# Gated delta rule in one block kernel: sums of squares in two other PSUM banks, the last level's mask ahead of the weights and the convolution

## The reference, cut to what matters

```python
qkv = silu(conv5(proj[..., C_QA:C_ZA]))            # depthwise, 5 taps
qa = _l2norm(q) * 128 ** -0.5 ; ka = _l2norm(k)    # x * rsqrt(sum(x*x) + EPS)
kb = kc * bc
a_kk = strict_lower(kb @ kc.T * gam)
sol = triangular_solve(a_kk + eye, [vc*bc, kb*exp(gc)])    # per chunk
...
o = _rmsnorm(o_forward + o_backward, norm_a) * silu(z)
```

## Time and profile before

| | us |
|---|---|
| median of the runs | 2743.36 |
| profiled execution, its own time | 2740.5 |
| its span | 2738.7 |
| TensorE busy in the span | 2316.0 (85%) |
| VectorE busy | 1069.8 (39%) |
| GpSimd busy | 828.6 (30%) |
| ScalarE busy | 705.8 (26%) |

### The profile page before, as it was taken

One profiled execution on the slowest core, in us unless ns is written; L12 is line 12 of the kernel. 1 busy time (PEld: TensorE's weight loads), 2 busy tenths in 40 slices (PEclk: granted clock), 3 DMA queues, 4 the chain that ended last, 5 costly groups with the idle time before them and its releaser, 6 DMA issues. The chain is left out here.

```text
span 2738.7 us, 30202 instructions
## 1 busy us (share of the span) xinstructions
PE 2316.0 (85%) x11455; PEld 1751.5 (64%) x11455; DVE 1069.8 (39%) x1761; ACT 705.8 (26%) x1088; POOL 828.6 (30%) x757
## 2 busy tenths in 40 slices
PE   4999778898869984999994996889997997479995
PEld 3888666776656663788883664678886666334442
DVE  3121356767730035433336453455664114311112
ACT  3333233334212122222222442422221212011110
POOL 2433045565412230544430111244441323000001
PEclk8999889999879997999997999899998999589998
DMA  4422123222004221323213303111101412759995
GB/s 132 107 77 62 35 76 91 62 56 76 24 14 125 81 92 46 123 92 107 92 46 68 78 16 105 35 31 24 25 7 26 133 47 97 312 201 419 417 418 202
DMA packets 283986, 292.86 MB, mean 107 GB/s; under 512 B 77552, under 2 KB 247664, under 8 KB 274224
## 3 DMA queue, kind: packets, MB, share of 16 engines
q1 hardware_dynamic: 271768, 240.58, 27.8%
q10 hardware_dynamic: 6816, 31.46, 2.8%
q0 software_dynamic: 5280, 19.18, 2.0%
HBM read 318.33 MB, written 23.17 MB: 125 GB/s over the span
## 5 line engine op out<-in xcount | busy, mean ns | idle before, releaser
L1983 PE MATMUL moe_bank<-ex_wgu,Y 128*64 128x512 f32 x768 | 171.4, 598 | 3.0 <-ACT Y L2030 1.6
L1352 POOL TENSOR_TENSOR m_wgs<-m_wg,m_wgs 128x1024 fp32r<-128x1024 f32 x32 | 79.4, 2499 | 251.1 <-ACT m_wgs L1388 251.1
L596 PE MATMUL gdn_bank<-hh,gdn_ws 128*128 128x512 f32 x256 | 119.0, 465 | 31.4 <-ACT gdn_rn L1081 24.4
L1983 PEld LDWEIGHTS moe_bank<-ex_wgu,Y 128*64 128x64 f32 x768 | 66.0, 138 | 103.3 <-issue 103.3
L1548 POOL TENSOR_TENSOR ff_wus<-ff_wu,ff_wus 128x2048 fp32r<-128x2048 f32 x16 | 73.8, 4610 | 185.9 <-ACT ff_wus L1606 185.9
L1433 DVE TENSOR_TENSOR m_sg<-m_sg,m_bank 128x512 f32<-128x512 f32 x32 | 22.0, 688 | 275.7 <-ACT m_sg L1396 275.7
L761 POOL TENSOR_TENSOR gdn_ws<-gdn_wr,gdn_ws 128x1024 fp32r<-128x1024 f32 x32 | 76.0, 2377 | 170.3 <-ACT gdn_ws L1032 170.1
L1955 POOL DMA_INDIRECT hT<-token_rows,rows x24 | 22.8, 951 | 344.9 <-PE moe_bank L1968 232.6
L596 PE MATMUL ff_bank<-ff_hh,ff_wus 128*128 128x512 f32 x256 | 101.0, 394 | 13.9 <-POOL ff_wus L1548 13.9
L596 PE MATMUL m_bank<-hh,m_wgs 128*128 128x512 f32 x256 | 106.1, 414 | 0.0
L597 PE MATMUL gdn_bank<-hl,gdn_ws 128*128 128x512 f32 x256 | 105.8, 413 | 0.0
(11 more groups left out here) (516 smaller groups left out, 5814.1 us busy)
## 6 DMA issues: line engine op xcount, KB each, us to landing
ex_wgu<-in_w_gate_e SPq DMA_DIRECT2D x42, 1024.0 KB, 16.5
ex_wgu<-in_w_up_e SPq DMA_DIRECT2D x42, 1024.0 KB, 19.3
ex_wd<-in_w_down_e SPq DMA_DIRECT2D x42, 1024.0 KB, 21.7
Y<-in_w_in SPq DMA_DIRECT2D x48, 512.0 KB, 3.9
gdn_wr<-in_w_in SPq DMA_DIRECT2D x32, 512.0 KB, 4.1
m_wg<-in_w_in SPq DMA_DIRECT2D x32, 512.0 KB, 5.6
ff_wu<-in_w_ff SPq DMA_DIRECT2D x16, 1024.0 KB
ff_wd<-in_w_ff SPq DMA_DIRECT2D x16, 1024.0 KB
```

The source lines that it names most:

```text
L596: pe.matmul(bank, left(0, l), right(0, r), start=(start and n == 0), stop=False)
L1352: pool.tensor_tensor(wgs[:, j, n, 1], wg[:, n], wgs[:, j, n, 0], ALU.subtract).then_inc(s.low, 1)
L1983: ins = pe.matmul(bank[2 + j][half, :], hgT[:, j, k, half], w[:, e, k], start=(k == 0), stop=(k == KT - 1))
```

## The change

The two sums of squares go to banks 4 and 5, which in a period's first third nobody uses, since the chain of the head before has left them. The output's sum of squares goes to bank 4. TensorE's `fill` for a first step in bank 0 then waits for VectorE's convolution of the head before, and in bank 1 for ScalarE's SiLU of z, both from the end of the period before, in place of ScalarE's Ln. The chain's first multiply in direction 1 waits for the Ln of both sums and of the norm. `gram_kq` moves behind `yz_mm(1)`. On VectorE, `take_yz(1)` and `take_x(2)` stand ahead of `weights` and of the first five taps. ScalarE's, GpSimd's and the DMA queue's orders stay.

```diff
@@ fill
                         if b == 0 and g:
-                            pe.wait_ge(s.rnl, 2 * g - 1)
-                        elif b == 1 and g >= 3:
-                            pe.wait_ge(s.orl, g - 2)
+                            pe.wait_ge(s.conv, 3 * g)
                         elif b == 1 and g:
-                            pe.wait_ge(s.rnl, 2 * g)
+                            pe.wait_ge(s.zs, g)
@@ squares(h)
                 pe.wait_ge(s.sq, 2 * h + 1)
-                pe.wait_ge(s.conv, 3 * h + 3)
-                pe.matmul(bank[0][:, :], G.c("ones"), sq[:, 0, :], start=True, stop=True).then_inc(s.ssq, 1)
+                if h == 0:
+                    pe.wait_ge(s.gts, 1)
+                elif h >= 2:
+                    pe.wait_ge(s.r, 6 * (h - 1))
+                    pe.wait_ge(s.vn, 8 * (h - 1))
+                pe.matmul(bank[4][:, :], G.c("ones"), sq[:, 0, :], start=True, stop=True).then_inc(s.ssq, 1)
                 pe.wait_ge(s.sq, 2 * h + 2)
-                pe.wait_ge(s.zs, h + 1)
-                pe.matmul(bank[1][:, :], G.c("ones"), sq[:, 1, :], start=True, stop=True).then_inc(s.ssq, 1)
+                pe.matmul(bank[5][:, :], G.c("ones"), sq[:, 1, :], start=True, stop=True).then_inc(s.ssq, 1)
@@ norm(j)
-                    pe.wait_ge(s.rnl, 2 * (j + 2) + 2)
-                pe.matmul(bank[1][:, :], G.c("ones"), osqb[:, :], start=True, stop=True).then_inc(s.oss, 1)
+                    pe.wait_ge(s.rnl, 2 * (j + 2) + 1)
+                else:
+                    pe.wait_ge(s.r, 6 * (j + 1))
+                pe.matmul(bank[4][:, :], G.c("ones"), osqb[:, :], start=True, stop=True).then_inc(s.oss, 1)
@@ chain, st = 0
+                            if d and h is not None:
+                                pe.wait_ge(s.rnl, 2 * h + 2)
+                            if d and i:
+                                pe.wait_ge(s.orl, i)
@@ TensorE's period
                     fill(g, 3)
+                if i is not None:
+                    yz_mm(i, 1)
                 if h is not None:
                     gram_kq(h)
-                if i is not None:
-                    yz_mm(i, 1)
                 fill(g, 4)
@@ ScalarE
-                        act.activation(rn[:, j, :], bank[j][:, :], ACT.Ln, bias=G.eps[:, 0:1]).then_inc(s.rnl, 1)
+                        act.activation(rn[:, j, :], bank[4 + j][:, :], ACT.Ln, bias=G.eps[:, 0:1]).then_inc(s.rnl, 1)
@@ VectorE's period
                 if i is not None:
                     take_x(i, 1)
+                if i is not None:
+                    take_yz(i, 1)
+                    take_x(i, 2)
                 if h is not None:
                     weights(h)
-                if i is not None:
-                    take_yz(i, 1)
                 convolve(5)
                 if i is not None:
-                    take_x(i, 2)
                     take_yz(i, 2)
                     chain(i)
```

More of the change, by code:

```diff
@@ L1088, in _ @@
                     act.wait_ge(s.oss, p)
-                    act.activation(ornb[:], bank[1][:, :], ACT.Ln, bias=G.eps[:, 0:1], scale=1.0 / P).then_inc(s.orl, 1)
+                    act.activation(ornb[:], bank[4][:, :], ACT.Ln, bias=G.eps[:, 0:1], scale=1.0 / P).then_inc(s.orl, 1)
                     act.wait_ge(s.orl, p)
```

## The result

The changed kernel takes 2749.55 us (median of 20 runs, 2743.71 to 2759.41) against 2742.84 us of the kernel before in the same comparison (20 runs): a ratio of 1.0023, 95% interval 1.0013 to 1.0032. It is some 6 us slower, 0.2%: less than the 8 us that the prediction took as its bound, and yet clear of no change.

A forecast was written before the change was run, and what follows sets the result against it. TensorE was taken to bound the kernel. Full periods -2.0, period p = -1 -2.2 and the clock +3.6 sum to -0.6 us, carried to the median of 2743.4: 2743 us, range 2731 to 2754.

The forecast's parts named there:

- the 8 us that the prediction took as its bound: Whole kernel's time: about 0.3% is what a measurement here can tell from no change.
- The exchange of waits: TensorE, full periods: three waits of 6.76 us become 0.7 (`gram_kk`), 0.7 (`x_mm(1)`), 2.0 (`yz_mm(1)`), 4.3 (`turn_v`); about 0.2 gained.
- VectorE's collision with GpSimd's split: VectorE's mask behind the taps: 2.77 us beside GpSimd's split, forecast to take the 0.69 it needs alone.
- Period p = -1: Period ahead of the full ones: first step no longer waits for Ln, `solve` starts earlier; -2.2 us, between 1.5 and 3.1.
- the tail: From p = 6 on: no gain, since its last head waits 5.1 us for the inverse by DMA, whose chain starts unchanged.
- +3.6 us for the clock: TensorE behind `turn_v`: clock falls as often as before, 13 us in all, of which 9.4 lay there before.
- the likeliest case: Whole kernel: waits are exchanged, no change, within -8 to +8 us; chance 0.67.
- -2.0: Six full periods without the clock term: -0.6, -0.9 and -0.5 us together; bounds +1.5 and -5.
- the upper bound of +9.3: TensorE's clock behind `turn_v`: the long fall every time, 6 x 3.1 = 18.7 us in place of 9.4.
- the taps that come later still: Rival: slower TensorE ahead of `take_x(2)` delays taps, SiLU, copy, `turn_v`; up to 1.7 us a period, +15 in all; chance 0.12.
- The prediction's row for the clock behind the wait for Ln: TensorE's granted clock behind that wait before the change: 1.00 four times, 0.66 over 5 us twice.

The follow-up runs named there:

- the idle matmuls: Changed kernel plus 7 matmuls nobody reads ahead of `yz_mm(1)` in the six full periods; ratio 1.0007 to the kernel before.
- the copies first: Changed kernel with ScalarE's `ktok` and `vtok` copies ahead of part k's SiLU and Square; ratio 0.9966 to the kernel before.
- the banks and the swap: Kernel before with the new banks and `gram_kq` behind `yz_mm(1)`, VectorE's order as before; ratio 1.0001, 2743.7 us.
- two steps early: Changed kernel with two of the four projection steps behind `gram_kq` moved ahead of `yz_mm(1)`; ratio 0.9965 to the kernel before, 2737.0 us.

## Why the prediction was wrong

*The exchange of waits* was right in its places and lengths: qT to mask 7.71 (7.69 forecast), waits of 0.65, 0.55, 1.85, 4.17 (0.7, 0.7, 2.0, 4.3), VectorE's collision with GpSimd's split gone, level 2's mask no longer late, no wait for Ln. With the clock held up by the idle matmuls, taps and `turn_v` are where the forecast has them, within 0.1 us.

*Period p = -1* gained 1.9 us of 2.2, *the tail* 2.8 where nothing was forecast. I don't have a cause for the latter; the tail is short of work and its clock differs from run to run.

*The step that failed* is the sentence "The new wait is longer, so I let the clock fall as often", and with it +3.6 us for the clock. It looked only at the wait at `turn_v`. At `yz_mm(1)` the likeliest case kept the full clock without a row for it. So the six periods were forecast at +1.6 us (-2.0 + 3.6) and measure +11.3, with 15.3 more of clock's loss. It has two parts. At `yz_mm(1)` the clock fell in five periods of six, and in the first one earlier: 1.46 us each on the path to the taps (4.14 - 2.68). Behind `turn_v` the long fall came every time (0.62 or 0.63 over 8 us, 3.0 us each, 18 in all), where the prediction had 13; that is close to the upper bound of +9.3 that it had worked out and had not taken.

The first part stood among the rivals, as the taps that come later still, at 1.7 us a period and a chance of 0.12. That rival is what happened, in mechanism and sign, but its sum was +15 and the result +6: the clock lost 15.3 us more where the rival has 19.5 (9.3 and 10.2), what is left of the six periods got 4 us shorter and not 2, and the tail 2.8. The measured 2749.55 us lies inside the range of 2731 to 2754, and even within the 8 us of the likeliest case. The latter is luck: the loss came from a place that this case left out, and savings that it had smaller or at nothing (4 us in the six periods, 2.8 in the tail) brought the total back under 8. One slip in the rival's own sum: -4.2 + 9.3 + 2 x 1.7 is 8.5, so it passes +8 from two such periods on and not from three.

The prediction's row for the clock behind the wait for Ln was also read too evenly. It speaks of a wait of 2.64 us, but in the six full periods that wait measured 3.04, 2.63, 2.64, 2.64, 3.58 and 3.47 us, and the clock fell behind the second 2.64 and the 3.58, and not behind 3.04 and 3.47. Length alone did not sort these waits even before the change.

Why a wait of 1.85 us brought the clock down each time in the changed kernel stays open. It isn't the length: the same wait left the clock at 1.00 in four of five periods with the copies first and in two of five with the banks and the swap. It isn't the sum of the waits just ahead either: the changed kernel has 0.65, 0.55 and 1.85, 3.05 us in all, and with the copies first p = 5 has 1.42, 0.53 and 1.84, 3.79 in all, and stays at 1.00. What the profile does show is that the five later periods of the changed kernel are alike to 0.05 us (54.61 to 54.66 each) and that the clock falls at the same point of each, 9.6 us after qT; before, they ran from 52.0 to 54.0. So these five falls are one case five times over and not five trials of a rule, and what the clock would do in a period of another length can't be read from them.

The rule of the Trainium skill (TensorE: Matmul & The Clock Gate, Part 1: The HAM clock gate) that was set beside the sum, that the engine goes to the half clock when it has stood idle, pointed to the upper bound behind `turn_v`; the trace agrees there. The fall behind 1.85 us is a case that no row of the kernel before would have given, and the measurement decides.

## What to carry to other kernels

When an engine with a clock gate loses one wait and gets others, the sum of the waits isn't the price. Here waits of one length, at one place, left the clock at 1.00 in one kernel and at half in the other. So work out each new wait that stands on the path to the next engine twice, with a fall of the clock and without one, and let the forecast carry both. A wait is cheapest where something useful can be moved into it: two steps moved ahead of a product were worth at least what seven idle matmuls were (312.3 and 315.4 us for the six periods). And take the parts of a change one at a time: here the new banks alone make the kernel 0.36% faster, and the reordering that went with them costs more than they bring. A reordering can cost by a dependency too: the swap by itself made `weights` late, and with it the masks behind it.

## What the runs showed of the hardware

Work that nobody reads made the program faster: 138 more matmuls in six periods, all inside waits, took the granted clock there from 0.90 to 0.99 and 16.8 us from these periods (about 18 from the time).

And a mask with two inputs in SBUF that starts beside a GpSimd product ended 0.55 us behind the end of that product, in all 17 cases of the changed kernel's delta rule too, so what it costs depends on how much of the product is left. In the kernel before it took 2.77 us against the split of 2.37 (ends at 539.07 and 538.52), with two steps early 1.81 us against a product of 1.29 (539.11 and 538.56). Where two products of some 1.3 us stand back to back it got in between them: in the changed kernel's period p = 2 the first mask took 1.33 us and ended while they still ran, and the second took 1.05 and ended 0.55 behind them (531.02 and 530.47), while the pair took 2.95 us and not 2.50 as in the kernel before:

```profile
527.52 2.95 POOL L812 TENSOR_TENSOR hT<-gdn_qT,gdn_gcB 128x512 f32<-128x512 f32 x2 [2.03 <-DVE gdn_qT L1190]
...
528.01 1.33 DVE L1177 TENSOR_TENSOR X<-X,const 128x512 f32<-128x512 f32 x1
...
529.97 1.05 DVE L1182 TENSOR_TENSOR X<-X,const 128x512 f32<-128x512 f32 x1
```
